# Seven instead of six seven-product slabs in two of the feed-forward networks, with five weight sums formed in device memory and two by VectorE

## What is computed

```python
x = x + 0.5 * swiglu_2(rms_norm(x, ffn1_norm[l]), ffn1_w_in[l], ffn1_w_out[l])
h = rms_norm(x, mix_norm[l]) @ w_mix_in[l]
...
x = x + y @ w_mix_out[l]
x = x + 0.5 * swiglu_2(rms_norm(x, ffn2_norm[l]), ffn2_w_in[l], ffn2_w_out[l])
...
def swiglu_2(h, w_in, w_out):
    gate, up = jnp.split(h @ w_in, 2, axis=-1)
    return (jax.nn.silu(gate) * up) @ w_out
```

## Time and profile before

| | |
|---|---|
| median of 3 runs | 1638.15 us (1638.14 to 1638.16) |
| profiled execution | 1637.92 us |
| its span, first to last instruction | 1636.6 us |
| TensorE busy | 1614.7 us, 99% |
| VectorE busy | 1237.8 us, 76% |
| ScalarE busy | 864.3 us, 53% |
| GpSimd busy | 343.6 us, 21% |
| mean granted TensorE clock | 1.000 |
| DMA | 380.81 MB, mean 233 GB/s |

### The profile page before, as it was taken

The page is one execution under the profiler, slowest core; times in us unless marked ns, Lnnn a source line. Parts: engine busy times, 40 slices in busy tenths (PEclk is TensorE's granted clock), DMA queues, the critical chain, the costliest instruction groups (busy, mean ns, idle before and its releaser), DMA issues.

```text
span 1636.6 us, 21299 instructions
## 1 busy us (share of the span) xinstructions
PE 1614.7 (99%) x7848; PEld 1304.6 (80%) x7848; DVE 1237.8 (76%) x1480; ACT 864.3 (53%) x1078; POOL 343.6 (21%) x501
## 2 busy tenths in 40 slices
PE   7999999999999999999999999999999999999999
PEld 3776788888778888788888888888888888888887
DVE  3898778897786764766888776679767988866687
ACT  3436654435475443544657554455544657564454
POOL 0002200001201231134403212441054304202350
PEclk9999999999999999999999999999999999999999
DMA  9788698898958876586675858758675784957763
GB/s 352 243 295 258 164 317 277 310 352 295 306 143 274 267 255 194 171 240 189 239 244 190 239 122 246 212 166 304 218 221 180 248 255 161 238 151 232 215 198 130
DMA packets 264118, 380.81 MB, mean 233 GB/s; under 512 B 17696, under 2 KB 198660, under 8 KB 264016
## 3 DMA queue, kind: packets, MB, share of 16 engines
q1 hardware_dynamic: 239744, 332.44, 61.6%
q0 software_dynamic: 21840, 42.51, 11.7%
q10 hardware_dynamic: 2432, 4.51, 0.8%
HBM read 363.92 MB, written 26.21 MB: 238 GB/s over the span
## 4 chain that ended last, share of the span: by engine, by line
PE 89%; DVE 5%; ACT 3%; issue 1%; DMA 1%; SPq 0%; DVEq 0%; ACTq 0%
PE bank L537 22%; PE bank L539 21%; PE bank L538 21%; PE bank L947 4%; PE bank L952 4%; PE bank L948 4%; DMA raw<-in_ada_w 1%; DVE lo L2113 1%; PE bank L1461 1%; PE bank L1462 1%; PE bank L1464 1%; PE bank L892 1%; PE bank L1269 1%; ACT hi L1517 1%; DVE XN L2577 1%
## 5 line engine op out<-in xcount | busy, mean ns | idle before, releaser
L2113 DVE TENSOR_TENSOR lo<-raw,hi 128x2048 fp32r<-128x2048 f32 x246 | 563.9, 2302 | 187.2 <-ACT hi L1517 186.0
L1517 ACT ACTIVATE hi<-raw 128x2048 fp32r<-128x2048 f32 x258 | 490.6, 1912 | 243.1 <-PE bank L539 146.9
L537 PE MATMUL bank<-hi,XTh 128*128 128x512 f32 (+1 forms) x1424 | 558.8, 392 | 1.7 <-DVE XTl L2248 1.3
L539 PE MATMUL bank<-hi,XTl 128*128 128x512 f32 (+1 forms) x1424 | 551.3, 387 | 0.0
L538 PE MATMUL bank<-lo,XTh 128*128 128x512 f32 (+1 forms) x1424 | 550.9, 387 | 0.0
L537 PEld LDWEIGHTS bank<-hi,XTh 128*128 128x128 f32 x1424 | 267.4, 188 | 66.0 <-issue 12.5
L539 PEld LDWEIGHTS bank<-hi,XTl 128*128 128x128 f32 x1424 | 267.4, 188 | 55.2
L538 PEld LDWEIGHTS bank<-lo,XTh 128*128 128x128 f32 x1424 | 267.5, 188 | 53.6 <-issue 1.0
L3200 POOL DMA_DIRECT2D HTR<-BLK x320 | 192.5, 610 | 490.3 <-DVE BLK L2673 416.3
L947 PE MATMUL bank<-hi,HTh 128*128 128x512 f32 x336 | 131.7, 392 | 0.0
L948 PE MATMUL bank<-lo,HTh 128*128 128x512 f32 x336 | 130.8, 389 | 0.0
(11 more groups left out here) (412 smaller groups left out, 2015.4 us busy)
## 6 DMA issues: line engine op xcount, KB each, us to landing
raw<-in_ffn_w_in SPq DMA_DIRECT2D x176, 512.0 KB, 4.9
raw<-in_ffn_w SPq DMA_DIRECT2D x132, 512.0 KB, 5.1
raw<-in_ada_w SPq DMA_DIRECT2D x96, 512.0 KB, 5.7
raw<-in_ffn_w_out SPq DMA_DIRECT2D x76, 512.0 KB, 4.2
raw<-in_w_mix_in SPq DMA_DIRECT2D x52, 512.0 KB, 4.9
sums<-in_ffn_w_out POOLq DMA_DIRECT2D x24, 512.0 KB, 8.9
raw<-in_od_pw_w SPq DMA_DIRECT2D x24, 512.0 KB, 7.5
raw<-sums SPq DMA_DIRECT2D x24, 512.0 KB, 4.8
```

The costliest lines, as they stand in the source:

```text
L537: pe.matmul(dst, xh, wh, start=start, stop=False)
L539: return pe.matmul(dst, xl, wh, start=False, stop=stop)
L1517: act.activation(hi[r][:, :], raw[g % RAW][:, :], ACT.Copy).then_inc(*up("hi", d))
L2113: dve.tensor_tensor(lo[r][:, :], raw[g % RAW][:, :], hi[r][:, :].bitcast(F32), ALU.subtract).then_inc(*up("lo", d))
```

## The change

In ffn(6) and ffn(8) seven slabs are formed with seven products instead of six: 0, 1, 2, 4, 5, 6 and 7 (before: 0, 1, 3, 4, 6 and 7). Stored sums are those of slabs 0, 2, 4, 5 and 7, and VectorE makes those of slabs 1 and 6. In the mixers GpSimd now forms the sums in groups of at most three slabs, so a second group of two follows the first, with waits of its own. The splits of moved chunks in the up phase of these two networks change places; those of the down phase stay. `LAST_COLUMNS` is 3 as before. Several helpers now take the number of the network instead of one list for all; code paths for a network 2 are added but not reached, as `FAST` has no entry for it. ffn(3) and ffn(5) keep their slabs and orders.

```diff
-FAST = (3, 5, 6, 8)
-FASTS = (0, 1, 3, 4, 6, 7)
-STORED = (0, 3, 6)
-FAST_SPLIT_UP = {5: (2,), 6: (0, 1), 8: (5,), 9: (3, 4)}
-FAST_SPLIT_DOWN = {1: (8,), 3: (6, 7), 4: (9, 10)}
-FAST_BATCH = {n: [i for i, s in enumerate(FASTS) if s in batch] for n, batch in enumerate(BATCHES[:3])}
+FAST = {p: (0, 1, 3, 4, 6, 7) for p in (3, 5, 6, 8)}
+STORED = {p: (0, 3, 6) for p in FAST}
+SPLITS = {p: ({5: (2,), 6: (0, 1), 8: (5,), 9: (3, 4)}, {1: (8,), 3: (6, 7), 4: (9, 10)}) for p in FAST}
+LAST_COLUMNS = {p: 3 for p in FAST}
+for _p in (6, 8):
+    FAST[_p], STORED[_p] = (0, 1, 2, 4, 5, 6, 7), (0, 2, 4, 5, 7)
+    SPLITS[_p] = {6: (0, 1), 7: (2,), 8: (3,), 9: (4, 5)}, {1: (8,), 3: (6, 7), 4: (9, 10)}
+BATCH = {p: [[i for i, s in enumerate(slabs) if s in batch] for batch in BATCHES[:3]] for p, slabs in FAST.items()}
 FAST_COLUMNS = {6: 0, 9: 1}
...
+        def stored_groups(p):
+
+            return [STORED[p][n:n + 3] for n in range(0, len(STORED[p]), 3)]
...
+                    if p in FAST and s == LAST_COLUMNS[p]:
+                        sums_high(p, 2)
+                    for n in (SPLITS[p][1] if p in FAST else SPLIT_DOWN).get(s, ()):
                         moved_high(n)
...
-                for i, s in enumerate(STORED):
-                    pool.dma_start(v[i][:, 0:D], w[s, 0, :, :]).then_inc(*up("sums_part", (p, s, 0), 16))
...
+                for group in stored_groups(p):
+                    for s in group:
+                        pool.dma_start(v[s][:, 0:D], w[s, 0, :, :]).then_inc(*up("sums_part", (p, s, 0), 16))
+                        pool.dma_start(v[s][:, D:SLAB], w[s, 1, :, :]).then_inc(*up("sums_part", (p, s, 1), 16))
+                    pool.wait_ge(*at("sums_part", (p, group[-1], 1)))
...
+                    pool.wait_ge(*at("sums_made", (p, group[-1])))
...
-                k0, k1 = 2 * FASTS[FAST_BATCH[n][0]], 2 * FASTS[FAST_BATCH[n][-1]]
-                step = max(k1 - k0, 1)
+                own = [2 * FAST[p][i] for i in BATCH[p][n]]
+                k0, k1, step = own[0], own[-1], own[1] - own[0] if len(own) > 1 else 1
...
                 if split in stored_at:
-                    sp.wait_ge(*at("sums_made", (stored_at[split], STORED[-1])))
+                    p, s = stored_at[split]
+                    sp.wait_ge(*at("sums_made", (p, next(group[-1] for group in stored_groups(p) if s in group))))
```

More of the change, by code:

```diff
@@ L477, in col @@
             return COLS[:, vec[name]:vec[name] + n]
[L479 removed]
+        A["sums"] = {p: nc.dram_tensor(f"sums{p}", (len(STORED[p]), P, SLAB), F32, kind="Internal").ap()
+                     for p in FAST if STORED[p]}
         slabs, first, dense, fast_at, stored_at, made_at = weight_slabs(A)
@@ L492, in down_at, with fast_batch, sums_slot, sums_own @@
         def down_at(p, s):
-            return first[f"down{p}"] + s + (sum(x < s for x in FASTS) if p - 1 in FAST else 0)
+            return first[f"down{p}"] + s + sum(x < s for x in FAST.get(p - 1, ()))
         def down_order(p):
-            kinds = [(s, (0, 1) if p - 1 in FAST and s in FASTS else (0,)) for s in range(DOWNS[p][0])]
+            kinds = [(s, (0, 1) if s in FAST.get(p - 1, ()) else (0,)) for s in range(DOWNS[p][0])]
             return [(down_at(p, s) + n, s, n) for s, parts in kinds for n in parts]
[L501 to L513, removed]
+        def fast_batch(p, i):
+            return next(n for n in range(3) if i in BATCH[p][n])
+        def sums_slot(p, i):
+            n = fast_batch(p, i)
+            return (i if len(FAST[p]) > 6 else (4, 6, 0)[n] + BATCH[p][n].index(i))
+        def sums_own(p, n):
+            i = BATCH[p][n][0]
+            return slice(sums_slot(p, i), sums_slot(p, i) + len(BATCH[p][n]))
+        def stored_groups(p):
+            return [STORED[p][n:n + 3] for n in range(0, len(STORED[p]), 3)]
         def sums_of(p):
@@ L894, in turn, with seven @@
                     last.then_inc(*up("turned", (p, t, h)))
-            def seven(f, d, s, i):
-                kk, batch = 2 * s, fast_batch(i)
-                begin, end = i == 0, i == len(FASTS) - 1
+            def seven(p, d, s, i):
+                f, kk, batch = FFNS[p], 2 * s, fast_batch(p, i)
+                begin, end = i == 0, i == len(FAST[p]) - 1
                 r, q = ready(d), (d + 1) % RING
@@ L932, in down @@
                 order = order or range(nslab)
+                normal = next(s for s in order if s not in FAST.get(p - 1, ())) if p else 0
                 def products(s, t, parts=(0, 1)):
@@ L2129, in shared_sums @@
                 dve.wait_ge(*at("e_part", (f, 1)))
-                dve.scalar_tensor_tensor(out=X[:, 0, :], in0=TR[:, 0:D], scalar=0.5, in1=X[:, 0, :], op0=ALU.mult,
-                                         op1=ALU.add).then_inc(*up("e_added", (f, 0)))
+                shared_added(f, 0)
                 dve.wait_ge(*at("e_part", (f, 2)))
@@ L2135, in shared_sums @@
                 dve.wait_ge(*at("e_part", (f, "last")))
-                dve.scalar_tensor_tensor(out=X[:, 1, :], in0=TR[:, D:SLAB], scalar=0.5, in1=X[:, 1, :], op0=ALU.mult,
-                                         op1=ALU.add).then_inc(*up("e_added", (f, 1)))
+                shared_added(f, 1)
             def split_first(d):
@@ L2716, in ffn @@
                             ada_quarter(*unit)
-                if during is not None and p not in FAST:
+                if during is not None and p != 3:
                     during()
@@ L3142, in weights_sums @@
[L3142 to L3148, removed]
```

100 lines of the change are left out of this document (58 added, 42 removed).

## The result

The changed kernel takes 1643.21 us (median of 7 runs, 1643.14 to 1643.28) against 1638.16 us for the kernel before (median of 7 runs beside it): ratio 1.0031, 95% interval 1.0021 to 1.0040, so 5.05 us slower. Its profiled execution took 1643.21 us with a span of 1641.9.

A forecast was written before the change was run, and what follows sets the result against it. TensorE bounds the kernel, with VectorE delivering just in time. New waits less fewer products and the old wait gave +2.40 in ffn(6) and +2.69 in ffn(8), together +5.09 us: forecast 1643.2 us, range 1640.2 to 1646.2.

The forecast's parts named there:

- the chain: Down phases: VectorE's work after slab 3's end delays slab 6's start and its sums; slab 6 ends 3.37 us late.
- The gain: Six products fewer on TensorE's path in the two down phases: 1.36 us less, 0.68 us in each.
- 0.29: Old wait of TensorE at slab 7's tenth product in ffn(6), kernel before: 0.29 us, claimed to go.
- The idle stretch and the ring: VectorE, done at about 1289.1, idles before slab 5's sums until TensorE leaves slab 3's ring place at 1291.26 us.
- this sign: In each down phase VectorE idles 3 us or more before slab 5's sums, ended by ScalarE, that by TensorE.
- second wait: TensorE waits for slab 6's sums, wanted 13.57 us after slab 3's end and ready at 14.81: 1.24 us.
- DMA: Two more stored slabs per down phase: share 0.80 to about 0.88, cost zero, bounds 0 and 2 us.
- Mixers: Second group of sums on GpSimd's queue ends at 992 to 1010; moves at most 0.2 us late: cost zero.
- No new wait: Rival: lo of slab 6's main split comes 1.9 us sooner, both waits vanish: -1.65 us, 1636.5; chance 0.12.
- half of it: Rival: the first wait at slab 6 comes, the second is covered: +2.4 us, 1640.5; chance 0.08.
- Clock: Rival: the new gaps lower TensorE's granted clock; four gaps cost 10.9 us, 1654; chance 0.02.
- GpSimd's queue: Rival: second group overruns 1010 by far more, ScalarE stands at 1036 for chunks: about 1646; chance 0.02.

The follow-up runs named there:

- the refitted run: Changed kernel with chunks 6 and 7 and the last column sums behind slab 2, chunks 9 and 10 behind slab 6: 1636.97 us.
- last chunks behind slab 5: Changed kernel with VectorE's HTl/HTh copies of chunks 9 and 10 placed behind slab 5 instead of slab 4: 1642.51 us.
- both: Changed kernel with chunks 6 and 7 and the last column sums behind slab 2, chunks 9 and 10 behind slab 5: 1637.88 us.
- main part first: Changed kernel with VectorE splitting slab 6's main part before it forms that slab's weight sums: 1649.55 us.
- the run that waited for it: Changed kernel with slab 6's weight sums formed by VectorE ahead of the split of slab 5's sums, in its idle stretch: 1641.85 us.
- seven stored: Changed kernel with all seven weight sums formed in device memory, in groups of three, three and one, none made by VectorE: 1670.8 us.

## Why the prediction was right

It said 1643.2 us by a sum of +2.40 for ffn(6) and +2.69 for ffn(8); measured were 1643.21 us and, apart, +2.42 and +2.63. That the total agrees to 0.01 us is luck: the median of the kernel before alone moves by 0.1 us from one set of runs to the next (1638.16 to 1638.27). What is not luck is the chain behind it.

- **The gain.** Six products fewer, as said. That they are worth 1.36 us was not measured apart, but the refitted run bears it out: 1.36 and 0.29 gained less two waits of 0.27 (with restart) is -1.11, measured -1.2.
- **The idle stretch and the ring.** Seen: VectorE waits before slab 5's sums, released by ScalarE, and that by slab 3. In ffn(8) it was 3.95 us, in ffn(6) 2.77 and not 3 or more, so this sign held in one phase and was missed by 0.23 us in the other. The prediction allowed ScalarE up to a microsecond for holding units up; in ffn(6) it was 1.6 by starts: VectorE stood 0.79 us for slab 2's main unit, behind a table load of 1.28 us on ScalarE, and 0.70 us for slab 5's, whose load ScalarE had waited for. The stretch absorbed it, so it cost nothing.
- **The chain.** In ffn(6) every point of the chain was within 0.02 us, counted from the end of slab 3, and moving 2.34 us of it into the idle stretch brought 4.6 us back. This is the run that shows the cause; the others show the size.
- **Starts, not durations.** Summed by the durations in the rows (0.69 and 2.29 us), the chain would have given 1644.4 by the prediction's 0.6 us a phase; added up again, it is 0.7 us, 1644.6. The link from one start to the next gave slab 6 within 0.01 us.
- **A link that was hidden.** The prediction's second wait took no account of ScalarE's hi of the made sums. It begins with the sums made and, with its hop, takes 2.1 us, while VectorE had 2.94 us of other work between (main split and chunks 9 and 10), so it did not show. The expectations of the three experiments that took cover away (last chunks behind slab 5, both, main part first) were too good for this reason, by 0.3 to 1 us a phase.
- **DMA.** Zero was right: no wait of TensorE in the phases is ended by a DMA. The load queue carried 3.15 MB more over the whole run (335.59 for 332.44), as four more stored slabs let expect (0.75 times 1,048,576 bytes each), but the share over the same 56 us went from 0.80 to 0.84 and not to about 0.88; why only half of it falls there stays open. Nor was there much room: in the run that waited for it, slab 6 landed at 1293.3 us in ffn(6), late in the 1283 to 1298 of the prediction.
- **Mixers.** Zero, shown apart. The second group issued its last step at 993 us, inside the predicted 992 to 1010 with its landing.
- **The rivals.** No new wait, and half of it: excluded by the waits. Clock: not in this kernel, but seen at gaps of 4.2 us, at 4.4 us for two gaps (2.7 and 1.7 with the restart, where the prediction had priced 2.7 each). GpSimd's queue: not in this kernel, but seen with seven stored.

## What to carry to other kernels

When a change moves work between slabs of a fixed program order, add up the operations between the event that lets the engine go on and the late product, by starts of consecutive operations, and compare with what the waiting engine has left to do; totals and busy shares said here that VectorE would be relieved. An idle stretch of the engine right ahead of such a chain is the sign that moving work can pay where saving it does not: one number in a table of places, with the one for the column sums, was worth 4.6 us, while the products it was about are worth 1.4. And for each link name the other engine's work that runs beside it, with its length, because it becomes the link when the cover is moved.

## What the runs showed of the hardware that was not expected

- In the run with the main part first, waits of 4.2 us of TensorE, with full clock before them, were followed by 13 and 11 products at a granted clock of 0.50 and 0.57, which lost 2.7 and 1.7 us; behind the waits of 1.88 and 1.25 us of the changed kernel it stayed at 1.00.
- After the waits that left the clock at 1.00 the first product takes 0.31 us to the next instead of 0.23, and the rest comes in hundredths: twelve products take 2.84 us instead of 2.72, so 0.12 us in all, whatever the length of the wait (0.15 to 1.9 us, in the kernel before, the changed one and the run with both moved).
- The time of a group of accumulating copies in device memory does not go with its size: with all seven stored, GpSimd took 54 us from the first group's first issue (905.24) to the next group's (959.50), 57 us to the third's (1016.54), and 32 us for the third's one slab (to 1049.06). Each has four steps that wait for each other. The mean DMA share was 0.85, 1.02 and 1.01 in these three stretches; how much of a group's time is steps and how much is other traffic no run shows.
